# State-space levels of a hybrid trunk: eight places of a hand-written timetable, or four

## The chip, the cores and the metric

The kernel runs on one core of a Trainium2 chip. The metric is the device time of one execution in microseconds. It was run three times on the chip, and the median is compared; one more execution was recorded by the hardware profiler. Engines: TensorE (PE, with its weight loads shown apart as PEld), VectorE (DVE), ScalarE (ACT), GpSimd (POOL) and SyncE (SP), which here only issues DMAs.

## The reference, cut to what matters

One layer over 1024 frames of width 2048: RMSNorm, one input projection, three groups of heads (A: HGRN2, 6 heads; B: band attention, 5; C: retention, 5), each with a SiLU gate, one output projection, a residual and a last RMSNorm. The change touches group A only:

```
o_inter = einsum('bhtk,bhkv->bhtv', qn * exp(b), state)        # b = cumsum(log f)
diff    = b[:, :, :, None, :] - b[:, :, None, :, :]
decay   = exp(where(causal[:, :, None], diff, -inf))
scores  = einsum('bhtsk,bhsk->bhts', qn[:, :, :, None, :] * decay, kn)
o       = o_inter + einsum('bhts,bhsv->bhtv', scores, vn)
new_state = exp(b_last)[..., None] * state + einsum('bhsk,bhsv->bhkv', kn * exp(b_last - b), vn)
```

The decay between two frames differs per channel, so the scores aren't one matrix product. They are built by halving: for a block of 2n frames, the scores of the late half against the early half are a product of q * exp(b - b_mid) and k * exp(b_mid - b), with b_mid the last frame of the early half.

## The kernel before

The work is staged in three parts. First 30 of the 59 tiles of the input projection, with seven products in place of eight (Strassen's scheme, to about 598 us), then the other 29 tiles one by one, with the heads' own work laid between their matmuls (to about 1460 us), then the output projection, again with seven products. Everything is float32; a projection is three matmuls of split values (high x high, low x high, high x low), 512 columns each.

In the middle part `project(g, stages)` walks through a tile of weights in 16 rows; after every second row, which is 12 matmuls of 512 columns, it calls one entry of a list `stages`. Such a place is a *slot*; a tile has 8. `put(slot, *parts)` hangs parts into a slot, and they run on TensorE one after the other at the slot's end. This list is the timetable. TensorE issues in order, so a part whose semaphores are not there holds up the whole projection.

A head of group A begins at slot b = -4 + 20 u, u = 0 to 5, and has these parts on TensorE:

- `a_diag`: the diagonal blocks, 32 products of 32x32 outputs (64 instructions in the trace, each float32 product being two), into PSUM `mix[1]`.
- `a_level(u, n)`, n = 0 to 5, for halves of 64, 32, 16, 8, 4, 2 frames. Level 0 has 64-column tiles (16 instructions), level 1 has 32-column tiles (32), levels 2 to 5 have 32-column tiles (64). Even levels write `mix[0]`, odd ones `mix[1]`. The operands are in `LV[n % 2]`, two buffers in SBUF.
- `a_near`: neighbours one frame apart, two matmuls of 512 columns with a matrix of ones over a split vector (`part_sums`, L843 and L844), into `mix[0]`.
- `a_kdtr`, `a_state`, `a_out`, `a_ss`: transposes (L832), chunk states (L900), output (L911, L914), sums of squares.

The other engines work through an order of their own. For each level n VectorE does, in `a_unit`:

```python
                for n in range(NM):
                    if n + 2 < NM:
                        lv_diff_of(u, n + 2)
                    if n == 4:
                        near_diff_of(u)
                    lv_drain(u, n)
...
                    if n == 3:
                        dve.wait_ge(z1_in, 16 * (2 * u + 2))
                        silu_clamp(2 * u + 1)
                    if n + 2 < NM:
                        lv_mult(u, n + 2)
```

`lv_diff_of(u, n + 2)` (L1792, L1793) waits until TensorE has finished level n, whose operands it overwrites; ScalarE then takes the exponential (L1136), and `lv_mult` (L1800, L1802) forms the operands of level n + 2. `lv_drain` (L1846 for levels 0 and 1, L1853 for the others) copies a level's blocks out of PSUM. At n = 4 follow `near_diff_of` (L1809), `near_mult` (L1815, L1817), `silu_finish` (L1657) and `part_low` (L1822); the near stage waits for the last. The clamp (L1648) starts ScalarE's sigmoid of the gate: three passes, with near's exponential behind them. After level 5's drain come `near_drain` (L1832), the start of the next head and, once `a_state` is done, the states.

GpSimd meanwhile splits each arriving granule of projection weights into a high and a low part (L765, L767). A granule serves two slots; SyncE loads the next into its place when TensorE has done with it.

Of the kernel before, what the change touches and what calls it, by code (L numbers as in the profile page):

```python
# [134 lines left out]
def build(nc, xT, wi, w, wo, gain, lbl, hgain, relb, fgain, ident_d, level_d, start_d, rot_d, dec_d, outT):  # L135
# [4 lines left out]
    with ExitStack() as ctx:  # L140
# [69 lines left out]
        def blocks(n):  # L210
            return arena[:, n, :].rearrange("p (c t) -> p c t", c=BLK)
# [63 lines left out]
        def mixb(n):  # L275
            return mix[n][:, :].rearrange("p (c t) -> p c t", c=BLK)
# [502 lines left out]
        def _(pe):  # L779
# [42 lines left out]
            def fill(n, before):  # L822

                if not (isinstance(before, int) and before == 0):
                    pe.wait_ge(drained[n], before)
# [13 lines left out]
            def part_sums(out, use):  # L839


                pe.wait_ge(parts_split, use + 1)
                nc.tensor.matmul(out, ones[:], part_hi[:], start=True, stop=False)  # L843
                return nc.tensor.matmul(out, ones[:], part_lo[:], start=False, stop=True)  # L844

            def a_diag(u):
                def stage():
                    pe.wait_ge(rstd_ready, 3)
                    pe.wait_ge(k_ready, u + 1)
                    pe.wait_ge(silu_done, 2 * u + 1)  # L850
                    fill(1, A_M1 * u)
                    for c in range(BLK):
                        for at in range(0, P, ROWS):
                            last = nc.tensor.matmul(mixb(1)[at:at + ROWS, c, at:at + ROWS],
                                                    blocks(K)[:, c, at:at + ROWS], blocks(Q)[:, c, at:at + ROWS],
                                                    start=True, stop=True)
                    last.then_inc(filled[1], 1)
                return stage

            def a_near(u):  # L860
                def stage():
                    fill(0, A_M0 * u + 3)
                    part_sums(mix[0][:, 0:HALF], A_PARTS * u).then_inc(filled[0], 1)
                return stage

            def a_level(u, n):
                def stage():
                    m = n % 2
                    pe.wait_ge(lv_ready, 2 * (NM * u + n + 1))
                    fill(m, (A_M0 * u + n // 2) if m == 0 else (A_M1 * u + 1 + n // 2))  # L870
                    size = LEVELS[n]
                    for c in range(BLK):
                        if n < WIDE:
                            for early in range(0, P, 2 * size):
                                late = early + size
                                out_row = early + size * (c % 2)
                                last = nc.tensor.matmul(
                                    mixb(m)[out_row:out_row + size, c, late:late + size],
                                    blocks(LV[n % 2])[:, c, early:early + size],
                                    blocks(LV[n % 2])[:, c, late:late + size], start=True, stop=True)  # L880
                        else:
                            for at in range(0, P, ROWS):
                                part = blocks(LV[n % 2])[:, c, at:at + ROWS]
                                last = nc.tensor.matmul(mixb(m)[at:at + ROWS, c, at:at + ROWS], part, part,  # L884
                                                        start=True, stop=True)
                    last.then_inc(filled[m], 1)
                return stage

            def a_kdtr(u):
                def stage():  # L890
                    transposes(1, T3, kd_ready, u + 1, A_M1 * u + 4)
                    a_vtr(u)
                return stage

            def a_state(u):
                def stage():
                    pe.wait_ge(drained[1], A_M1 * u + 5)
                    pe.wait_ge(drained[0], A_M0 * u + 5)
                    for c in range(BLK - 1):
                        last = nc.tensor.matmul(mixb(1)[:, c, :], blocks(KDT)[:, c, :],  # L900
                                                blocks(V)[:, c, :], start=True, stop=True)
                    last.then_inc(filled[1], 1)
                return stage

            def a_out(u):
                def stage():
                    pe.wait_ge(drained[1], A_M1 * u + 6)
                    pe.wait_ge(qe_ready, u + 1)
                    fill(0, A_M0 * u + 5)
                    for c in range(BLK):  # L910
                        last = nc.tensor.matmul(mixb(0)[:, c, :], blocks(V)[:, c, :],  # L911
                                                blocks(SC)[:, c, :], start=True, stop=(c == 0))
                        if c > 0:
                            last = nc.tensor.matmul(mixb(0)[:, c, :], blocks(ST)[:, c, :],  # L914
                                                    blocks(QE)[:, c, :], start=False, stop=True)
                    last.then_inc(filled[0], 1)
                return stage
# [10 lines left out]
            def a_ss(u, half):  # L928
                return sum_squares(1, A_PARTS * u + 1, half, A_M1 * u + 6)
# [114 lines left out]
            def put(slot, *parts):  # L1044
                before = stages[slot]

                def stage():
                    before()
                    for part in parts:
                        part()  # L1050
                stages[slot] = stage

            for u in range(A_HEADS):
                b = A_FROM + A_EACH * u
                put(b + 7, a_diag(u))
                put(b + 8, a_level(u, 0))
                put(b + 9, a_level(u, 1))
                put(b + 11, a_level(u, 2))
                put(b + 12, a_level(u, 3))
                put(b + 13, a_level(u, 4))  # L1060
                put(b + 15, a_level(u, 5))
                put(b + 16, a_near(u))
                put(b + 17, a_kdtr(u))
                put(b + 18, a_state(u))
                put(b + 20, a_out(u))
                put(b + 22, a_ss(u, 0))
                put(b + 24 if u < A_HEADS - 1 else b + 23, a_ss(u, 1))
            for i in range(B_HEADS):
                b = B_FROM + B_EACH * i
# [3 lines left out]
            for i in range(C_HEADS - 1):  # L1073
                b = C_AT[i]
# [1265 lines left out]
```

## Time and profile before

| what | value |
| --- | --- |
| median of 3 runs | 1789.6 us (1788.89 to 1789.95) |
| profiled execution, its own time | 1790.76 us |
| its span, first to last instruction | 1789.0 us |
| mean granted TensorE clock | 0.993 of full speed |
| TensorE busy | 1745.5 us, 98% |
| VectorE busy | 1211.0 us, 68% |
| GpSimd busy | 766.8 us, 43% |
| ScalarE busy | 670.4 us, 37% |
| DMA, mean rate | 181 GB/s |

An engine that is busy for nearly all of the span sets the time; the others matter where that one waits for them. Matmuls overlap in the array, so the sum of their single durations is more than the busy time, and start-to-start distances are what prices a piece of work.

### The profile page before, as it was taken

What the parts mean: (1) busy time and instruction counts of PE and PEld (TensorE: products, weight loads), DVE (VectorE), ACT (ScalarE), POOL (GpSimd) and SP (SyncE); (2) the same over time, 40 slices, a digit from 0 to 9 for tenths busy, and PEclk for the clock granted to TensorE, in tenths of its full rate; (3) what the DMA queues carried; (4) which work ended last, traced back from release to release, by engine and by line L of the source; (5) the groups of instructions that cost most, each with busy time, mean ns of one, the idle gap of its engine ahead of it and who ended that gap; (6) DMA issues with size and microseconds to landing.
All of it is one profiled execution on the core that took longest, in us unless ns stands there. A gap on an engine that the chain in (4) does not pass through costs nothing.

```text
span 1789.0 us, 26920 instructions
## 1 busy us (share of the span) xinstructions
PE 1745.5 (98%) x10330; PEld 1443.2 (81%) x10330; DVE 1211.0 (68%) x1714; ACT 670.4 (37%) x972; POOL 766.8 (43%) x545
## 2 busy tenths in 40 slices
PE   7999999999999899999999999999999999999996
PEld 5888888888888788888887888888888877888884
DVE  6857565564678987787787356555655457778987
ACT  4423334332434253343443233332543223333442
POOL 4544444444455644444444333333333450354541
PEclk9999999999999999999999999999999999999997
DMA  7767777685987433224223332323433378778876
GB/s 247 228 229 252 242 239 255 218 269 184 301 270 247 153 99 109 89 84 123 85 84 124 108 108 84 106 84 106 145 109 110 97 247 307 234 241 261 287 241 223
DMA packets 160851, 323.29 MB, mean 181 GB/s; under 512 B 18378, under 2 KB 19151, under 8 KB 160724
## 3 DMA queue, kind: packets, MB, share of 16 engines
q1 hardware_dynamic: 146458, 276.52, 48.4%
q10 hardware_dynamic: 14266, 45.05, 7.3%
q8 instruction: 83, 1.36, 0.3%
q14 instruction: 44, 0.36, 0.1%
HBM read 275.35 MB, written 46.15 MB: 180 GB/s over the span
## 4 chain that ended last, share of the span: by engine, by line
PE 57%; DVE 5%; DMA 2%; issue 1%; ACT 1%; SPq 0%; POOL 0%; ACTq 0%; DVEq 0%
PE prj L813 33%; PE prj L1095 13%; PE mix L958 2%; PE mix L941 1%; DMA y_in<-y_scratch 1%; PE mix L832 1%; DVE arena L2276 1%; PE mix L951 1%; PE mix L884 1%; PE mix L911 1%; PE mix L914 1%; PE mix L900 1%; PE mix L989 0%; PE mix L1011 0%; DVE w_lo L2221 0%
## 5 line engine op out<-in xcount | busy, mean ns | idle before, releaser
L765 POOL TENSOR_SCALAR w_hi<-w_sum 128x512 fp32r<-128x512 f32 x124 | 198.9, 1604 | 514.2 <-DMA w_sum<-in_w 494.8
L792 PE MATMUL prj<-in_hi,w_hi 128*128 128x512 f32 x840 | 329.5, 392 | 10.7 <-DVE w_lo L1687 8.9
L792 PE MATMUL prj<-in_lo,w_hi 128*128 128x512 f32 x840 | 328.3, 391 | 0.0
L792 PE MATMUL prj<-in_hi,w_lo 128*128 128x512 f32 x840 | 328.2, 391 | 0.0
L813 PE MATMUL prj<-mv_hi,w_hi 128*128 128x512 f32 x928 | 300.6, 405 | 0.0
L752 POOL TENSOR_TENSOR w_sum<-in_raw,in_raw 128x512 f32<-128x512 f32 x150 | 200.0, 1334 | 214.4 <-PE prj L792 203.3
L813 PE MATMUL prj<-mv_lo,w_hi 128*128 128x512 f32 x928 | 288.4, 392 | 0.0
L813 PE MATMUL prj<-mv_hi,w_lo 128*128 128x512 f32 x928 | 286.4, 390 | 0.0
L813 PEld LDWEIGHTS prj<-mv_hi,w_lo 128*128 128x128 f32 x928 | 174.5, 188 | 38.8
L813 PEld LDWEIGHTS prj<-mv_lo,w_hi 128*128 128x128 f32 x928 | 174.5, 188 | 38.4
L792 PEld LDWEIGHTS prj<-in_hi,w_hi 128*128 128x128 f32 x840 | 158.5, 189 | 45.8 <-issue 9.4
L1687 DVE TENSOR_TENSOR w_lo<-w_sum,w_hi 128x512 fp32r<-128x512 f32 x150 | 119.0, 795 | 110.3 <-ACT w_hi L1198 108.4
L813 PEld LDWEIGHTS prj<-mv_hi,w_hi 128*128 128x128 f32 x928 | 163.9, 189 | 28.5 <-issue 0.9
L792 PEld LDWEIGHTS prj<-in_hi,w_lo 128*128 128x128 f32 x840 | 158.5, 189 | 33.3
L792 PEld LDWEIGHTS prj<-in_lo,w_hi 128*128 128x128 f32 x840 | 158.5, 189 | 33.1 <-issue 0.5
L774 POOL TENSOR_TENSOR raws<-raws 128x512 f32<-128x512 f32 x80 | 111.9, 1401 | 164.8 <-DMA raws<-in_wo 164.8
L1095 PE MATMUL prj<-mv_hi,w_hi 128*128 128x512 f32 x448 | 175.4, 391 | 6.4 <-POOL w_lo L767 4.1
L1136 ACT ACTIVATE arena<-arena 128x1024 f32<-128x1024 f32 (+1 forms) x121 | 123.6, 1034 | 151.2 <-DVE arena L1793 127.0
L767 POOL TENSOR_TENSOR w_lo<-w_sum,w_hi 128x512 fp32r<-128x512 f32 x124 | 173.8, 1402 | 10.3
L1095 PE MATMUL prj<-mv_lo,w_hi 128*128 128x512 f32 x448 | 174.4, 389 | 0.0
L1095 PE MATMUL prj<-mv_hi,w_lo 128*128 128x512 f32 x448 | 174.3, 389 | 0.0
L1198 ACT ACTIVATE w_hi<-w_sum 128x512 fp32r<-128x512 f32 x150 | 94.1, 628 | 178.2 <-POOL w_sum L752 178.0
(177 smaller groups left out, 2473.5 us busy)
## 6 DMA issues: line engine op xcount, KB each, us to landing
in_raw<-in_wi SPq DMA_DIRECT2D x360, 256.0 KB, 3.2
raws<-in_wo SPq DMA_DIRECT2D x184, 256.0 KB, 3.5
w_sum<-in_w SPq DMA_DIRECT2D x116, 256.0 KB, 2.9
arena<-z_scratch ACTq DMA_DIRECT2D x56, 512.0 KB, 4.0
y_in<-y_scratch SPq DMA_DIRECT2D x80, 256.0 KB, 4.5
z_scratch<-acc_in SPq DMA_DIRECT2D x60, 256.0 KB, 4.0
z_scratch<-stage SPq DMA_DIRECT2D x26, 512.0 KB, 4.2
x_even<-in_xT SPq DMA_DIRECT2D x44, 256.0 KB, 3.9
```

The lines of the kernel that those rows point to most:

```text
L752: nc.gpsimd.tensor_tensor(w_sum[wslot(n)][:], in_raw_buf(a), in_raw_buf(b), ALU.add if sign > 0 else ALU.subtract).then_inc(in_wsum, 1)
L765: nc.gpsimd.tensor_scalar(w_hi[q][:], w_sum[q][:], 1.0, None, ALU.mult).then_inc(w_hi_done, 1)
L767: nc.gpsimd.tensor_tensor(w_lo[q][:], w_sum[q][:], w_hi[q][:].bitcast(F32), ALU.subtract).then_inc(w_split, 1)
L774: nc.gpsimd.tensor_tensor(raw_buf(a), raw_buf(a), raw_buf(b), ALU.add if sign > 0 else ALU.subtract).then_inc(wsum_done, 1)
L792: last = nc.tensor.matmul(out, wt[wslot(n)][:, i % GRAN, :], mv[j % 2][:, i, :], start=(i == 0 and wt is w_hi and mv is in_hi), stop=(i == ...
L813: last = nc.tensor.matmul(prj[pair][:, half(side)], wt[wslot(q)][:, kk, :], mv[:, k, half(side)], start=(k == 0 and wt is w_hi and mv is m ...
L832: last = nc.tensor.transpose(mixb(n)[:, c, :], blocks(src)[:, c, :], ident[:])
L958: last = nc.tensor.matmul(mixb(1)[:, 5, :], blocks(V)[:, p + 1 - nk + j, :], blocks(BT[p % 2])[:, j, :], start=(j == 0), stop=(j == nk - 1))
L1095: last = nc.tensor.matmul(bank(s), wt[wslot(W0 + n)][:, i % GRAN, :], slot(mv, j, i), start=(i == 0 and wt is w_hi and mv is mv_hi), stop= ...
L1136: return nc.scalar.activation(out, src, ACT.Exp, **kw)
L1198: nc.scalar.activation(w_hi[wslot(n)][:], src, ACT.Copy).then_inc(in_w_hi, 1)
L1687: tt(w_lo[wslot(n)][:], src, w_hi[wslot(n)][:].bitcast(F32), ALU.subtract).then_inc(w_split, 1)
```

## The change

The eight parts of each head, from the diagonal to near, keep their order and their content. They are hung into fewer slots: the diagonal with level 0, level 1 with 2, level 3 with 4, level 5 with near, three slots apart. Nothing else of the kernel is edited.

```diff
             for u in range(A_HEADS):
                 b = A_FROM + A_EACH * u
-                put(b + 7, a_diag(u))
-                put(b + 8, a_level(u, 0))
-                put(b + 9, a_level(u, 1))
-                put(b + 11, a_level(u, 2))
-                put(b + 12, a_level(u, 3))
-                put(b + 13, a_level(u, 4))
-                put(b + 15, a_level(u, 5))
-                put(b + 16, a_near(u))
+                put(b + 7, a_diag(u), a_level(u, 0))
+                put(b + 10, a_level(u, 1), a_level(u, 2))
+                put(b + 13, a_level(u, 3), a_level(u, 4))
+                put(b + 16, a_level(u, 5), a_near(u))
                 put(b + 17, a_kdtr(u))
                 put(b + 18, a_state(u))
                 put(b + 20, a_out(u))
```

## Rows read from the trace of the kernel before

**Rows 1.** The page: busy us, share of the span and instructions of an engine.
```profile
PE 1745.5 (98%) x10330; PEld 1443.2 (81%) x10330; DVE 1211.0 (68%) x1714; ACT 670.4 (37%) x972; POOL 766.8 (43%) x545
```

**Rows 2.** TensorE's waits: for whom, us in total, times, longest.
```profile
PE mix L884 <- DVE arena L1802: 4.6, 2, 3.0
```

**Rows 3.** Windows: length, busy of PE, PEld, DVE, ACT, POOL; clock, DMA share, GB/s.
```profile
618.00:621.00 3.00, 0.02 (x1) 0.00 (x0) 3.00 (x4) 0.00 (x0) 2.92 (x3) 0.96 0.00 0
621.00:623.00 2.00, 1.97 (x66) 1.78 (x67) 2.00 (x2) 0.00 (x0) 1.63 (x2) 0.50 0.00 0
728.00:797.00 69.00, 69.00 (x677) 56.67 (x676) 53.35 (x72) 27.73 (x31) 30.38 (x20) 1.00 0.30 93
```

**Rows 4.** The chain of work that ended last: start, us, three slots of projection.
```profile
803.57 8.16 PE prj L813 x36
```

**Rows 5.** Timeline of weight loads, head 3, then level 3 of head 4: start, duration.
```profile
811.65 0.65 PEld L854 LDWEIGHTS mix<-arena 128*32 128x32 f32 x64 [0.35 <-issue]
815.31 0.55 PEld L877 LDWEIGHTS mix<-arena 128*64 128x64 f32 x16 [0.35 <-issue]
818.87 0.35 PEld L877 LDWEIGHTS mix<-arena 128*32 128x32 f32 x32 [0.35 <-issue]
824.93 0.65 PEld L884 LDWEIGHTS mix<-arena 128*32 128x32 f32 x64 [0.35 <-DVE arena L1802]
828.59 0.65 PEld L884 LDWEIGHTS mix<-arena 128*32 128x32 f32 x64 [0.35 <-issue]
832.25 0.65 PEld L884 LDWEIGHTS mix<-arena 128*32 128x32 f32 x64 [0.35 <-issue]
838.63 0.65 PEld L884 LDWEIGHTS mix<-arena 128*32 128x32 f32 x64 [0.35 <-issue]
841.97 0.19 PEld L843 LDWEIGHTS mix<-part_hi,ones 128*128 128x128 f32 x1
...
897.28 0.65 PEld L884 LDWEIGHTS mix<-arena 128*32 128x32 f32 x64 [0.35 <-issue]
```

**Rows 6.** Timeline of VectorE, head 3, from level 3's end to near.
```profile
829.48 1.10 DVE L1792 TENSOR_TENSOR arena<-arena 128x512 f32<-128x512 f32 x1
...
832.35 0.67 DVE L1648 TENSOR_SCALAR arena<-arena 128x1024 f32<-128x1024 f32 x1
...
836.86 0.69 DVE L1815 TENSOR_TENSOR arena<-arena 128x512 f32<-128x512 f32 x1 [0.77 <-ACT arena L1136]
837.58 1.66 DVE L1817 TENSOR_TENSOR arena<-arena 128x512 f32<-128x512 f32 x1
...
840.30 0.68 DVE L1822 TENSOR_TENSOR part_lo<-arena,part_hi 128x512 fp32r<-128x512 f32 x1
```

**Rows 7.** Timeline of VectorE, head 1, the same stretch, first and last.
```profile
692.52 0.68 DVE L1792 TENSOR_TENSOR arena<-arena 128x512 f32<-128x512 f32 x1
...
703.59 0.68 DVE L1822 TENSOR_TENSOR part_lo<-arena,part_hi 128x512 fp32r<-128x512 f32 x1
```

**Rows 8.** Timeline of VectorE, head 0, the same stretch, first and last.
```profile
625.70 0.69 DVE L1792 TENSOR_TENSOR arena<-arena 128x512 f32<-128x512 f32 x1
...
635.17 0.68 DVE L1822 TENSOR_TENSOR part_lo<-arena,part_hi 128x512 fp32r<-128x512 f32 x1
```

**Rows 9.** Timeline of weight loads, head 0: levels 2, 3, 4 and near.
```profile
614.30 0.65 PEld L884 LDWEIGHTS mix<-arena 128*32 128x32 f32 x64 [2.04 <-DVE arena L1802]
621.03 0.95 PEld L884 LDWEIGHTS mix<-arena 128*32 128x32 f32 x64 [3.44 <-DVE arena L1802]
625.95 0.65 PEld L884 LDWEIGHTS mix<-arena 128*32 128x32 f32 x64 [0.35 <-DVE arena L1802]
...
635.97 0.19 PEld L843 LDWEIGHTS mix<-part_hi,ones 128*128 128x128 f32 x1 [0.33 <-issue]
```

**Rows 10.** Timeline of GpSimd, head 3: one half of each of two weight splits.
```profile
829.02 1.89 POOL L765 TENSOR_SCALAR w_hi<-w_sum 128x512 fp32r<-128x512 f32 x1 [3.19 <-DMA w_sum<-in_w]
...
837.17 1.52 POOL L767 TENSOR_TENSOR w_lo<-w_sum,w_hi 128x512 fp32r<-128x512 f32 x1
```

## The prediction

> **What bounds the kernel now.** I read the page's busy table first. TensorE is busy for 98% of the span [rows 1], so the time is TensorE's queue plus its waits. The view of the waits, for TensorE alone, then says how much of them belongs to the six A heads: only 4.6 us in two waits, both ahead of a level (L884) and both for VectorE's multiply L1802 [rows 2]. The windows show one whole head, 728 to 797 us: TensorE has work for 69.00 of 69.00 us at full clock, VectorE for 53.35 [rows 3]. So in heads 1 to 5 each microsecond in which TensorE issues or waits more is a microsecond of the total; in head 0 it is VectorE that leads.
>
> The timeline of weight loads prices a stage. A slot of projection is 8.16 / 3 = 2.72 us [rows 4]. From the diagonal blocks to level 0 is 3.66 us, from level 3 to level 4 is 3.66, from level 4 over two slots to level 5 is 6.38 [rows 5]: a stage of 64 small matmuls adds 0.94. Level 1 has 32 and adds 824.93 - 818.87 - 5.44 = 0.62. So a small matmul costs 0.01 us and the stage, as a stage, 0.30. Each of them starts with an idle 0.35 on the loader, for 128x32 tiles and for 128x64 ones alike; the near stage, on the whole array, starts with none [rows 5].
>
> **The change, part by part.** No instruction, transfer or buffer is added or removed. What is issued where changes on TensorE only; the orders on VectorE, ScalarE, GpSimd and SyncE's queue stay. Against the head's start b: level 0 moves from b+8 to b+7, level 1 from b+9 to b+10 (later), level 2 from b+11 to b+10 (earlier), level 3 from b+12 to b+13 (later), level 4 stays, level 5 moves from b+15 to b+16 (later), near stays.
>
> *Gain.* Levels 1 and 2 follow each other with the same tile shape, as do 3 and 4: each seam saves the 0.30 of a stage. Level 5 and near save nothing, since near never paid. The diagonal and level 0 differ in shape (128x32, then 128x64), and no row has such a pair: nothing saved is one bound, 0.30 the other. The idle 0.35 appears whenever the array goes from whole to narrow tiles and must come from the shape, since the near stage waits on semaphores too and has none; I take 0.10, near the lower bound, because the tile shape changes here as well. (The Trainium skill, "TensorEngine Tiling (Array Packing)", Key Properties, says that changing the tiling mode drains TensorE. By that rule the seam saves nothing and the sum ends 0.5 us higher; with the row's price counted as fully saved it would be 1.0 us lower. The idle 0.35 ahead of narrow stages agrees with the rule.)
>
> *What the later levels cost.* VectorE's queue is in order. Behind its wait for level 3 stand: the differences for level 5 (L1792, L1793), level 3's drain, the clamp L1648, the products for level 5, near's difference L1809, level 4's drain, near's products L1815 and L1817, the gate L1657 and the split L1822. TensorE's near stage waits for the last of these. I call the stretch from L1792 to the end of L1822 the chain. It took 840.98 - 829.48 = 11.50 us in head 3 [rows 6], 704.27 - 692.52 = 11.75 in head 1 [rows 7] and 635.85 - 625.70 = 10.15 in head 0 [rows 8]. Between the start of level 3 and near TensorE had 13.38 us before [rows 5]: the chain starts 0.89 after level 3, ends 12.39 after it in head 3, and fits.
>
> Now near comes after level 3 by: 0.64 (level 3's matmuls) + 0.94 (level 4 as a stage) + 8.16 (three slots) + 0.62 (level 5; 841.97 - 838.63 - 2.72) = 10.36 us. The chain needs 0.89 + 10.15 + 0.12 = 11.16 at its shortest (0.12: from the chain's end to near's start in head 0 [rows 8, 9]). So near waits in every head: at least 0.8 us.
>
> How long is the chain? Of the 4.51 us from the clamp to L1815 [rows 6], all is ScalarE's (three passes for the sigmoid, one for near); the VectorE work under it has 3.7 us and so 0.8 us of slack. The rest, 5.6 us, is plain VectorE work that GpSimd's splits of the projection weights stretch: L1792 took 1.10 instead of 0.69 beside L765 [rows 6, 10], L1817 took 1.66 instead of 0.69 beside L767, and began anew only when L767 was through at 838.69. GpSimd's pair starts some 3.4 us after an odd slot frees its weights. Level 3 will stand right behind an odd slot, so a pair falls 3 to 6 us into the stage, mostly under ScalarE's part: it costs what exceeds the slack, I take 0.4. The next falls 10 us in, on the gate or the split: 0.3. Chain: 10.15 + 0.7 = 10.85. Bounds: 10.15 (no collision) and 11.75 (as head 1).
>
> *Sum for a head.* From near to the next head's level 3 it was 897.28 - 841.97 = 55.31 [rows 5]; it becomes 55.31 + 2.72 - 0.30 - 0.10 = 57.63. From there to near 0.89 + 10.85 + 0.12 = 11.86, a wait of 1.5. The period is 69.49 instead of 68.69 (897.28 - 828.59): +0.80. The seam between levels 3 and 4 is inside the wait and is worth nothing.
>
> *Head 0.* VectorE is busy for 3.00 of 3.00 us while level 3 waits [rows 3, 9], and it has level 1 and level 2 as early as it needs them in either order. Level 2 will wait some 5 us in one piece at 609 to 614 us instead of 1.7 and 3.1 in two, and level 4 will start when the products for it are done, 625.9 as now [rows 9]. Its near at 635.97 was already set by the chain. So head 0 keeps its time: 0 (from -1.1, if a weight split misses VectorE, to +0.4).
>
> Five periods from near to near: 5 x 0.80 = +4.0 us. After head 5's near every stage stands at its old slot, and near's drain and level 5's end ahead of the transposes a slot later, so the shift is passed on whole. The profiled execution took 1790.8 us (span 1789.0), 1.2 over the median of the runs: 1789.6 + 4.0 = 1793.6.
>
> Other waits checked: level 4 needs the products for it, 7.96 us after level 1 starts (VectorE: 0.55, then three steps of each of two levels at 1.2 to 1.35), and comes after 10.0; a collision or two fit. If not, level 4 is later and near's wait shorter by as much. Level 2 needs its own 5.5 us after the diagonal and comes after 9.9.
>
> **The rivals.**
> 1. *The chain meets no weight split.* 10.15 us, +0.10 a head, +0.5 in all: 1790.1. For it: head 0 ran so. Against it: all of heads 1 to 5 were longer, and a pair of splits comes with every second slot.
> 2. *The chain is as long as before.* 11.75: +1.70 a head, 1798.1. For it: five heads had 11.5 to 11.8. Against: level 3 now stands elsewhere against the splits.
> 3. *The wait pulls the clock down.* In head 0 a wait of 3.1 us was followed by a granted clock of 0.50 for 621 to 623 us [rows 3, 9], and the slot behind it took 4.92 instead of 3.66: 1.26 lost. The wait of 1.7 us at 614.30 cost no clock. Near's wait would be 1.5, but idle 0.3 and a stage of small matmuls stand right ahead of it. If it counts, 5 x 1.26 more: 1799.9.
> 4. *Faster: near doesn't wait.* If what near needs were ready within 10.36 us of level 3, the three seams would be pure gain: 5 x 0.9 = 4.5, 1785.1. It decides at a chain of 9.35 us, 0.8 below the shortest one seen.
> 5. *Nothing changes*, because a stage's 0.30 isn't lost at its boundaries but in its matmuls: then the period is 0.4 longer than in the forecast, 1795.6.
>
> **How the numbers follow.** About 0.2% (3.6 us) is what a measurement of this kernel can tell from no change. Forecast, a chain of 10.5 to 11.3: 0.60, with a range of its own of 1791.8 to 1796; rival 1: 0.15; rival 2: 0.08; rival 3: 0.07; rival 4: 0.05; rival 5: 0.05. 1793.6 lies just beyond 0.2% (1793.2), so of the forecast 0.34 is slower and 0.26 the same. Slower: 0.34 + 0.08 + 0.07 + 0.05 = 0.54. Same: 0.26 + 0.15 = 0.41. Faster: 0.05. The range from 1789.8 to 1798.5 leaves out rivals 3 and 4 and the better end of rival 1.
>
> **What would show it.** In the profile after, for heads 1 to 5: a start-to-start of 0.3 us from level 1 to level 2 and 0.6 from 3 to 4, with no idle between; some 0.5 to 0.8 from the diagonal to level 0; TensorE waiting at near's first matmul (L843) for L1822, five times 0.8 to 2.4 us; a period of 69.5; level 2 of head 0 waiting 5 us. Wrong it would be if the chain were under 10.2, if the waits stood at level 4 instead, or if the granted clock left 1.00 in the heads.

## The result, and the profile after

The changed kernel takes 1798.07 us (median of 5 runs, 1796.48 to 1800.84), the kernel before 1789.95 (5 runs, 1788.89 to 1793.3). The ratio is 1.0046, with a 95% interval from 1.0035 to 1.0057: 8.1 us slower, where the forecast was 4.0 us slower. The profiled execution took 1797.53 us, its span is 1795.7.

The waits of TensorE alone, in the kernel after (line, for whom, us in total, times, longest). Lines of the file behind the timetable stand four earlier than before: L1818 is L1822 of before, L1798 is L1802.

```profile
PE mix L843 <- DVE part_lo L1818: 9.5, 6, 3.0
PE prj L792 <- DVE w_lo L1683: 8.2, 1, 8.2
PE mix L884 <- DVE arena L1798: 5.9, 1, 5.9
```

The first row did not exist before: near now waits in each of the six heads. The second belongs to the start of the kernel and was 8.9 us before. The third is head 0; the 4.6 us in two waits of [rows 2] have become 5.9 in one.

The timeline of weight loads in head 4, to be held against [rows 5]:

```profile
884.74 0.65 PEld L854 LDWEIGHTS mix<-arena 128*32 128x32 f32 x64 [0.35 <-issue]
885.43 0.55 PEld L877 LDWEIGHTS mix<-arena 128*64 128x64 f32 x16
894.43 0.35 PEld L877 LDWEIGHTS mix<-arena 128*32 128x32 f32 x32 [0.35 <-issue]
894.67 0.70 PEld L884 LDWEIGHTS mix<-arena 128*32 128x32 f32 x64
903.82 1.25 PEld L884 LDWEIGHTS mix<-arena 128*32 128x32 f32 x128 [0.35 <-issue]
913.50 0.65 PEld L884 LDWEIGHTS mix<-arena 128*32 128x32 f32 x64 [0.35 <-issue]
915.89 0.19 PEld L843 LDWEIGHTS mix<-part_hi,ones 128*128 128x128 f32 x1 [1.75 <-issue]
```

All three seams are free of the idle 0.35. Near starts 2.39 us after level 5, where 0.64 would do: 1.75 us of waiting, though the row calls it "issue" and only the view of the waits names L1818. (Single waits at near are given below as this idle time of the loader; the view of the waits has them 0.1 us shorter.) From level 3 to near it is 12.07 us.

What near waits for, on VectorE in the same head, to be held against [rows 6]:

```profile
904.62 0.69 DVE L1788 TENSOR_TENSOR arena<-arena 128x512 f32<-128x512 f32 x1 [1.59 <-PE mix L884]
...
907.05 1.12 DVE L1644 TENSOR_SCALAR arena<-arena 128x1024 f32<-128x1024 f32 x1
...
909.30 1.78 DVE L1805 TENSOR_TENSOR arena<-arena 128x512 f32<-128x512 f32 x1
...
912.23 0.67 DVE L1811 TENSOR_TENSOR arena<-arena 128x512 f32<-128x512 f32 x1
...
914.68 1.10 DVE L1818 TENSOR_TENSOR part_lo<-arena,part_hi 128x512 fp32r<-128x512 f32 x1
```

And GpSimd beside it, to be held against [rows 10]:

```profile
907.02 1.62 POOL L765 TENSOR_SCALAR w_hi<-w_sum 128x512 fp32r<-128x512 f32 x1 [2.85 <-DMA w_sum<-in_w]
908.73 1.81 POOL L767 TENSOR_TENSOR w_lo<-w_sum,w_hi 128x512 fp32r<-128x512 f32 x1
914.03 2.08 POOL L765 TENSOR_SCALAR w_hi<-w_sum 128x512 fp32r<-128x512 f32 x1 [3.49 <-DMA w_sum<-in_w]
```

Ahead of the chain VectorE now stands idle for 1.59 us until level 3 is through; then it has 915.78 - 904.62 = 11.16 us of work in one piece, in which three operations are stretched: the clamp (1.12 instead of 0.67) by L765, near's difference (1.78 instead of 0.67) by L767, the split (1.10 instead of 0.68) by the next L765.

The granted clock fell in two waits of TensorE and stayed at 0.50 behind them, at near of head 1, which starts at 707.18, and at level 2 of head 0, at 613.11 (columns as in [rows 3]):

```profile
707.00:709.00 2.00, 1.79 (x4) 1.49 (x5) 1.84 (x5) 0.00 (x0) 0.00 (x0) 0.50 0.69 244
709.00:711.00 2.00, 2.00 (x7) 1.55 (x6) 1.97 (x5) 0.00 (x0) 0.00 (x0) 0.67 0.02 6
...
612.00:615.00 3.00, 1.89 (x66) 1.74 (x67) 2.94 (x7) 0.71 (x1) 3.00 (x1) 0.50 0.02 5
615.00:617.00 2.00, 2.00 (x6) 1.52 (x6) 1.96 (x4) 0.35 (x1) 1.92 (x3) 0.50 0.00 0
```

Where the 6.7 us between the two spans lie, by four starts on TensorE, each read from the timeline of weight loads:

| stretch | before | after | difference |
| --- | --- | --- | --- |
| start to the diagonal of head 0 | 599.34 | 597.03 | -2.3 |
| from there to near of head 0 | 36.63 | 39.36 | +2.7 |
| near of head 0 to near of head 5 | 343.39 | 348.40 | +5.0 |
| from there to the end | 809.6 | 810.9 | +1.3 |

The change touches nothing in the first stretch. Over the profiled executions of all the kernels below it ran from 596.7 to 599.4, and the last one from 806.8 to 813.8: both vary by more than what they show here. So the two middle rows, 7.7 us, are what the change did in this trace, and the 8.1 us of the medians agree.

### The profile page after: what moved, and what is told of

Read it like the earlier page. It is cut to its first block, busy times and chain, and to the rows that moved or that the text cites. A ratio compares the mean times of both kernels' runs of the same rounds, so it can differ in the third digit from the quotient of the medians.

```text
span 1795.7 us, 26920 instructions
## 1 busy us (share of the span) xinstructions
PE 1741.8 (97%) x10330; PEld 1446.3 (81%) x10330; DVE 1203.7 (67%) x1714; ACT 669.2 (37%) x972; POOL 778.1 (43%) x545
## 4 chain that ended last, share of the span: by engine, by line
PE 54%; DVE 7%; issue 2%; DMA 2%; ACT 1%; SPq 0%; POOL 0%; ACTq 0%; DVEq 0%
PE prj L813 30%; PE prj L1091 13%; PE mix L958 2%; PE mix L941 1%; PE mix L832 1%; DVE arena L2272 1%; PE mix L951 1%; DMA y_in<-y_scratch 1%; ACT arena L1132 1%; PE mix L911 1%; PE mix L914 1%; PE mix L900 1%; PE mix L1011 0%; PE mix L989 0%; PE mix L884 0%
## 5 line engine op out<-in xcount | busy, mean ns | idle before, releaser
L765 POOL TENSOR_SCALAR w_hi<-w_sum 128x512 fp32r<-128x512 f32 x124 | 202.5, 1633 | 516.5 <-DMA w_sum<-in_w 497.1
L752 POOL TENSOR_TENSOR w_sum<-in_raw,in_raw 128x512 f32<-128x512 f32 x150 | 203.8, 1359 | 208.3 <-PE prj L792 197.9
L1683 DVE TENSOR_TENSOR w_lo<-w_sum,w_hi 128x512 fp32r<-128x512 f32 x150 | 114.9, 771 | 110.1 <-ACT w_hi L1194 107.4
L767 POOL TENSOR_TENSOR w_lo<-w_sum,w_hi 128x512 fp32r<-128x512 f32 x124 | 175.2, 1413 | 10.3
```

The lines of the kernel that those rows point to most:

```text
L752: nc.gpsimd.tensor_tensor(w_sum[wslot(n)][:], in_raw_buf(a), in_raw_buf(b), ALU.add if sign > 0 else ALU.subtract).then_inc(in_wsum, 1)
L765: nc.gpsimd.tensor_scalar(w_hi[q][:], w_sum[q][:], 1.0, None, ALU.mult).then_inc(w_hi_done, 1)
L767: nc.gpsimd.tensor_tensor(w_lo[q][:], w_sum[q][:], w_hi[q][:].bitcast(F32), ALU.subtract).then_inc(w_split, 1)
L1683: tt(w_lo[wslot(n)][:], src, w_hi[wslot(n)][:].bitcast(F32), ALU.subtract).then_inc(w_split, 1)
```

## The experiments

Each was timed beside the kernel before on the same chip. The lines of the timetable are those of the changed kernel if nothing else is said. For each the table gives what the traces show; a stage of 64 small matmuls added 0.90 us in these executions instead of 0.94, so the 343.39 of before answers to about 342.5 here, as the two controls have it. The new timetable shows no such difference: from near to the next head's level 3 it is 57.4 us in the changed kernel's own trace and in head0_old.

| kernel | diagonal to near, head 0 | near of head 0 to near of head 5 | near's waits, heads 1 to 5 | chain, mean of heads 1 to 5 | ratio to before (95%) |
| --- | --- | --- | --- | --- | --- |
| before | 36.63 | 343.39 | 0 | 11.69 | 1 |
| changed | 39.36 | 348.40 | 5 | 11.09 | 1.0046 (1.0035 to 1.0057) |
| level3_back | 37.57 | 340.38 | 0 | 11.21 | 0.9990 (0.9978 to 1.0002) |
| level3_only | 38.02 | 348.33 | 5 | 10.87 | 1.0049 (1.0032 to 1.0066) |
| gate_early | 38.34 | 339.89 | 1 | 9.36 | 0.9989 (0.9978 to 1.0001) |
| gate_early_before | 38.24 | 342.47 | 0 | 10.72 | 0.9997 (0.9985 to 1.0008) |
| head0_old | 36.62 | 347.17 | 5 | 11.11 | 1.0026 (1.0016 to 1.0037) |
| small_splits | 37.16 | 342.22 | 5 | 10.13 | 0.9978 (0.9968 to 0.9988) |
| small_splits_before | 32.46 | 342.46 | 0 | 10.16 | 0.9947 (0.9934 to 0.9960) |
| head0_level2 | 39.00 | 347.53 | 5 | 11.20 | 1.0049 (1.0033 to 1.0066) |
| best | 36.81 | 339.88 | 1 | 9.42 | 0.9981 (0.9972 to 0.9990) |

**Level 3 back by one slot.**

```diff
-                put(b + 13, a_level(u, 3), a_level(u, 4))
+                put(b + 12, a_level(u, 3))
+                put(b + 13, a_level(u, 4))
```

> The changed kernel with level 3 of each head put back one slot (b+12), level 4 alone at b+13. Theory (the VectorE chain from level 3's end to near's split sets near, and moving level 3 one slot later is what made near wait): near's waits in heads 1 to 5 go away, the seams diagonal/level 0 and level 1/level 2 stay, a period from near to near of 68.69 - 0.25 - 0.36 = 68.1 us instead of the 69.7 mean after, head 0 still loses about 2 us. Total about 1789 to 1792, some 6 to 9 us below the changed kernel. Rival (two levels back to back on TensorE cost by themselves, wherever they stand): only the seam between levels 3 and 4 is gone, about 1795 or more.

1790.11 us (12 runs). The waits at near are gone from the view of the waits, and the period is 68.02 to 68.11 us in all five heads, as expected. Head 0 loses 0.9 us, where about 2 were expected. In head 1:

```profile
690.93 0.65 PEld L884 LDWEIGHTS mix<-arena 128*32 128x32 f32 x64 [0.35 <-issue]
694.55 0.65 PEld L884 LDWEIGHTS mix<-arena 128*32 128x32 f32 x64 [0.35 <-issue]
703.61 0.65 PEld L884 LDWEIGHTS mix<-arena 128*32 128x32 f32 x64 [0.35 <-issue]
704.38 0.19 PEld L843 LDWEIGHTS mix<-part_hi,ones 128*128 128x128 f32 x1
```

13.45 us from level 3 to near, over a chain that is as long as in the changed kernel (a mean of 11.21 beside 11.09). The rival, that two levels in a slot cost by themselves, is refuted: two of the seams are still there and are a gain of 2 us over the control's 342.5. (The pair of levels 3 and 4 stands again in gate_early below, and costs nothing there.) In the total this gain can't be told from none, with head 0's loss beside it.

**Only level 3 moved**, in the kernel before:

```diff
-                put(b + 12, a_level(u, 3))
-                put(b + 13, a_level(u, 4))
+                put(b + 13, a_level(u, 3), a_level(u, 4))
```

> The kernel before with one edit alone: level 3 of each head one slot later, at b+13 with level 4. Theory: this alone brings near's waits. From near to the next level 3 58.0 us, from there to near about 12.0, a period of 70.0 instead of 68.7, 5 x 1.3 = 6.5 us slower than before, about 1796; head 0 keeps its two smaller waits at levels 2 and 3 and loses little. Rival (the loss comes from levels 1 and 2 in one slot): no wait at near, within 1 us of before.

1799.56 us (6 runs). One part moved by one slot gives as large a loss as the whole change. TensorE waits at near in heads 1 to 5, 5.7 us by the view of the waits, and the periods are 68.95 to 70.18. The size was missed: about 6.5 us were expected, and the ratio is worth 8.8. In the trace the five periods have 348.3 - 342.5 = 5.8 of it and head 0 1.4, where TensorE waits 4.0 us at level 4 and the granted clock is 0.50 behind that wait.

```profile
694.55 1.25 PEld L884 LDWEIGHTS mix<-arena 128*32 128x32 f32 x128 [0.35 <-issue]
701.55 0.65 PEld L884 LDWEIGHTS mix<-arena 128*32 128x32 f32 x64 [0.35 <-issue]
706.79 0.19 PEld L843 LDWEIGHTS mix<-part_hi,ones 128*128 128x128 f32 x1 [1.97 <-issue]
```

**The gate's clamp and sigmoid earlier.** On VectorE the clamp moves from level 3's step to level 1's, on ScalarE the sigmoid from behind level 5's exponential to ahead of it:

```diff
-                    if n == 3:
+                    if n == 1:
                         dve.wait_ge(z1_in, 16 * (2 * u + 2))
                         silu_clamp(2 * u + 1)
...
-                sigmoid(2 * u + 1)
+                    if n == 4:
+                        sigmoid(2 * u + 1)
```

> The changed kernel, with the gate's clamp on VectorE moved from level 3's step to level 1's, and the gate's sigmoid on ScalarE moved ahead of level 5's exponential. The same work, but 4.5 us of ScalarE's are no longer between the clamp and near's products. Theory: the chain from level 3's end to near's split falls to about 8.7 to 9.5 us, near no longer waits (it has 9.4), and the seams become pure gain, 0.95 a head: period 67.7, 5 us faster than before; head 0 gets back some 1 to 2 us. Total 1784 to 1788. Rival (near waits because VectorE is short of time, not for the path through ScalarE): the chain stays near 11 us and the total near 1798.

1788.39 us (11 runs). The chain is 9.1 us in four heads and 10.40 in head 3, the only one of the five in which near waits (0.98 us). VectorE in head 1, the whole chain:

```profile
694.52 0.70 DVE L1789 TENSOR_TENSOR arena<-arena 128x512 f32<-128x512 f32 x1 [1.01 <-PE mix L884]
695.15 0.67 DVE L1790 TENSOR_TENSOR arena<-arena 128x512 f32<-128x512 f32 x1
695.76 1.32 DVE L1850 COPY_PREDICATED arena<-level,mix 128x1024 f32<-128x1024 int8 x1
...
697.02 0.69 DVE L1797 TENSOR_TENSOR arena<-arena 128x512 f32<-128x512 f32 x1
697.63 1.10 DVE L1799 TENSOR_TENSOR arena<-arena 128x512 f32<-128x512 f32 x1
698.65 0.68 DVE L1806 TENSOR_TENSOR arena<-arena 128x512 f32<-128x512 f32 x1
699.26 1.34 DVE L1850 COPY_PREDICATED arena<-level,mix 128x1024 f32<-128x1024 int8 x1
...
700.49 0.67 DVE L1812 TENSOR_TENSOR arena<-arena 128x512 f32<-128x512 f32 x1
701.20 0.69 DVE L1814 TENSOR_TENSOR arena<-arena 128x512 f32<-128x512 f32 x1
701.81 1.22 DVE L1654 SCALAR_TENSOR_TENSOR arena<-arena 128x1024 f32<-128x1024 f32 x1
702.94 0.69 DVE L1819 TENSOR_TENSOR part_lo<-arena,part_hi 128x512 fp32r<-128x512 f32 x1
```

Near starts at 704.13 right behind level 5, half a microsecond after the split is there. With the gate taken out of the chain, it fits under three slots: from head 0's near to head 5's it is 8.5 us shorter than in the changed kernel (7.3 shorter than in head0_old, where the clock does not fall), and the seams are now a gain. What left the chain is not only the path through ScalarE. In heads 1, 3 and 4 of the changed kernel VectorE has no wait for ScalarE at near's products (L1811); there the clamp itself is gone, 1.0 to 1.1 us, and the splits meet near's difference in head 3 alone (1.78; 0.68 above). In heads 2 and 5 a wait of 0.38 and 0.34 is gone as well. The edit moves both halves of the gate, so these runs don't price them singly. The part of the expectation on head 0 was nearly right: 38.34 after 39.36, 1.0 us back where 1 to 2 were expected. The sum was not reached: the total was to be 5 us faster than before and at most 1788.0 us, and by its interval the median can't be told from the kernel before.

The same edit in the kernel before, as the control:

> The kernel before with the same move of the gate's clamp and sigmoid, the timetable untouched. Theory: near does not wait in the kernel before, so a shorter chain is worth nothing: the period stays 68.7, within 1 us of before. Rival (the gate's place costs something of its own): it moves by more than 2 us, and then the run of the changed kernel with this edit can't be read as the timetable's gain.

1790.87 us (12 runs), no difference from before: the periods are 68.49 to 68.50 and near has no wait to lose. In head 0, where VectorE leads, the earlier clamp stands ahead of level 3's products: level 3 comes 0.7 us later, the clock stays low for longer behind its wait, and the head takes 1.6 us more (38.24). So what gate_early gains over this control, 2.6 us of 342.5 in the heads, is the timetable's.

**Head 0 alone on the old timetable** (eight `put` lines of before for u = 0, the four of after for the others).

> The changed kernel, but head 0 alone keeps the eight places of before. Theory (head 0 loses because its one wait of 5.5 us at level 2 is followed by a low clock that makes level 3 late for VectorE): from the diagonal to near 36.6 us in head 0 instead of 39.35, the other heads as in the changed kernel, total 2 to 3 us below it, about 1795 to 1797. Rival (head 0's difference is only its weight splits falling elsewhere): it stays at 38 or more.

1795.84 us (12 runs): head 0 takes 36.62 us, exactly as before, and the total is 0.20% of the kernel's time nearer to before (ratios 1.0026 and 1.0046), as expected. So the change costs head 0 2.7 us in the trace, and heads 1 to 5 the rest. All five wait at near, 1.18 to 1.88 us, and in none of them the granted clock leaves 1.00: the sum is 347.2 - 342.5 = 4.7 us.

**GpSimd's operations cut to a sixteenth.** This kernel and its control leave out work: of each granule of the middle part GpSimd treats 8 of 128 columns of each row, and the third product of the projection reads the high part of the weights, so the 29 tiles are computed with wrong weights.

```diff
-                nc.gpsimd.tensor_scalar(w_hi[q][:], w_sum[q][:], 1.0, None, ALU.mult).then_inc(w_hi_done, 1)
+                few = slice(0, P) if n < IN_GRANULES + NG or n >= W0 else slice(0, 8)
+                nc.gpsimd.tensor_scalar(w_hi[q][:, :, few], w_sum[q][:, :, few], 1.0, None, ALU.mult).then_inc(w_hi_done, 1)
...
-                    for wt, mv in ((w_hi, mv_hi), (w_hi, mv_lo), (w_lo, mv_hi)):
+                    for third, wt, mv in ((0, w_hi, mv_hi), (0, w_hi, mv_lo), (1, w_hi, mv_hi)):
```

> The changed kernel with GpSimd's two operations on the weights of the middle part cut to 8 of 128 columns a row; the third product of the projection reads the high part instead of the low one, so all 29 tiles of the middle part are computed with wrong weights, with the same matmuls. Theory (weight splits stretch the chain from 10.15 to 11.07 on average): all five chains 10.0 to 10.3 us, near's wait 0.7 to 0.9 each, near to near about 68.5 to 68.7 a head and no low clock, 5 us less than the changed kernel from head 0's near to head 5's. Rival (collisions aren't what differs between the chains): they still spread from 10.1 to 12.4.

1787.45 us (12 runs). The six chains are 10.12 to 10.15 us long, as head 0's of [rows 8]; near waits 0.67 to 0.71 in each head, the periods are 68.42 to 68.47, both at or just under the low end of what was expected. The five periods are 6.2 us shorter than in the changed kernel, where 5 were expected, and 5.0 shorter than in head0_old. In head 1, the chain's ends:

```profile
692.96 0.69 DVE L1789 TENSOR_TENSOR arena<-arena 128x512 f32<-128x512 f32 x1 [2.00 <-PE mix L885]
...
699.92 0.69 DVE L1812 TENSOR_TENSOR arena<-arena 128x512 f32<-128x512 f32 x1 [0.71 <-ACT arena L1133]
...
702.39 0.69 DVE L1819 TENSOR_TENSOR part_lo<-arena,part_hi 128x512 fp32r<-128x512 f32 x1
```

ScalarE ends later than VectorE here (0.71 us of waiting at near's products): without collisions the path through the sigmoid sets this part of the chain. In the changed kernel it does so in heads 2 and 5 only, and in heads 1, 3 and 4 VectorE's own stretched work does. All that the six chains differ by is GpSimd's work beside them.

> The same cut of GpSimd's operations in the kernel before, as a control. Theory: near has room there, so the period stays 68.5 to 68.7 in heads 1 to 5; head 0, which VectorE leads, shortens by 2 to 4 us from diagonal to near. Rival: heads 1 to 5 shorten as well, and then the splits cost TensorE something else.

1782.51 us (6 runs). Heads 1 to 5 keep 342.46, so the splits cost TensorE nothing where the chain has room. Head 0 falls from 36.63 to 32.46. Against this control the change costs heads 1 to 5 nothing (342.22) and head 0 4.7 us, and the two medians differ by 4.9.

The pair says something of head 0 too. Its chain is as short in both, 10.15 and 10.14 us, and still the change costs it 4.7 us. TensorE and VectorE at its level 3, in small_splits:

```profile
612.00 0.95 PEld L885 LDWEIGHTS mix<-arena 128*32 128x32 f32 x64 [4.30 <-DVE arena L1799]
623.71 1.25 PEld L885 LDWEIGHTS mix<-arena 128*32 128x32 f32 x128 [0.35 <-issue]
...
624.52 0.69 DVE L1789 TENSOR_TENSOR arena<-arena 128x512 f32<-128x512 f32 x1 [3.95 <-PE mix L885]
```

Behind a wait of 4.2 us the clock stands at 0.50 for 612 to 617 us, level 3 follows level 2 after 11.71 us instead of the 9.13 of the other heads, and VectorE stands idle for 3.95. So no collision is needed for head 0 to lose: a late level 3 is enough.

**Level 2 of head 0 one slot later.**

```diff
-                put(b + 10, a_level(u, 1), a_level(u, 2))
+                put(b + 10, a_level(u, 1))
+                put(b + 11 if u == 0 else b + 10, a_level(u, 2))
```

> The changed kernel with level 2 of head 0 alone put one slot later (b+11), so that TensorE has 2.7 us of projection to do before it waits for it. Theory (in head 0 the long wait at level 2 lowers the clock, level 3 comes 2.2 us late and VectorE, ready 1.7 us earlier, waits for it): the wait falls from 5.7 to about 3 us, at most 1.3 us are lost to the clock, level 3 is there before VectorE is, the VectorE wait of 1.7 us for it is gone and the diagonal-to-near time of head 0 falls from 39.35 to about 37.7 us, up to 1 us either way by where weight splits fall. Rival (only the weight splits differ): it stays above 39.

1798.48 us (4 runs), and 39.00 us from diagonal to near: the expected 37.7 was missed. VectorE's wait for level 3 is gone, as the theory has it, but what was to follow did not:

```profile
615.58 0.76 PE L884 MATMUL mix<-arena 128*32 128x32 f32 x64 [2.81 <-DVE arena L1799]
616.27 1.12 PE L813 MATMUL prj<-mv_hi,w_hi 128*128 128x512 f32 x2
617.18 1.05 PE L813 MATMUL prj<-mv_lo,w_hi 128*128 128x512 f32 x2
```

The wait of 2.8 us lowered the clock like the one of 5.9 (0.50 for 617 to 619 us); VectorE was through with the products for level 4 1.5 us later than in the changed kernel, counted from the diagonal, of which about 1.1 are operations that weight splits stretched; and TensorE waited another 2.8 us at level 4 and lost clock again behind it. That the old timetable cures head 0 is shown, and by small_splits that it loses without collisions too; how the 2.7 us of the changed kernel divide between a late level 3 and the splits is not.

**The version that these runs point to**: the four places and the early gate for heads 1 to 5, head 0 as in the kernel before.

```diff
-                    if n == 3:
+                    if n == (1 if u > 0 else 3):
```

and the same condition at the sigmoid (4 or 5).

> Heads 1 to 5 with the four places and the gate's clamp and sigmoid early, head 0 with everything as before. Theory: head 0 36.6 us from diagonal to near, a period of 67.8 in the others, near waiting at most once; 0.9 x 5 = 4.5 us faster than before, about 1785 to 1787. Rival (what is gained in the heads is given back behind them): below 1 us faster.

1787.88 us (12 runs) beside 1791.75 for the kernel before: 0.19% faster, the interval from 0.10 to 0.28%. The periods are 67.8, 68.7 in head 3. Expected were 4.5 us; in the heads the trace has 342.5 - 339.9 = 2.6, by the controls, and the medians differ by 3.9. The miss is in the price of the seams: with no wait a period is 67.79 instead of 68.49, so the new places are worth 0.7 a head and not 0.9, and head 3 loses more than that in a wait of 1.0.

## Why the prediction was right, point by point

The direction, the place and the cause of the loss were right. The size was not: 8.1 us instead of 4.0. The range held by 0.4 us (1798.07, its end is 1798.5), and that is partly luck: the end was set for a longer chain (rival 2), and what filled the difference are two terms that the sum had at nothing, head 0 (2.7 us) and one fall of the clock (1.4).

- *Near waits for VectorE's chain in every head, since level 3 comes one slot later.* Right, and shown from both sides: level3_back takes the waits away, level3_only brings them by itself, and a chain of 9.1 us (gate_early) makes them vanish, where the prediction had put the turning point at 9.35; the one head with a longer chain there (10.40) waits.
- *The chain, 10.85 us between 10.15 and 11.75.* Measured 12.48, 10.14, 11.05, 11.16 and 10.60, mean 11.1. The shortest agrees with the lower bound; head 1 went over the upper one, because five of its operations were stretched. The collisions were the unknown, taken as 0.7, and are 0.9. The forecast had the clamp free of them; it was stretched by up to 0.45 in three heads, ahead of ScalarE's part, where nothing hides it.
- *The seams, 0.30 + 0.10 outside the wait.* Level 2 now starts 0.25 us after level 1, where level 1 had been priced at 0.62: 0.36 saved, of which level 2 gives 0.04 back. The diagonal and level 0 follow at 0.69 us without the idle 0.35, and that saves 0.25. (The Trainium skill, "TensorEngine Tiling (Array Packing)", Key Properties, has any change of the tiling mode drain TensorE. This trace shows no such cost for 128x32 to 128x64: the idle 0.35 came only from the whole array to narrow tiles.) With 0.07 for level 5 and near, which the forecast had at nothing, it was 57.4 us from near to the next level 3, not 57.63.
- *The clock.* The forecast left it out of near's waits and gave it a rival of its own, with 0.07. It came once of five: in head 1, behind a wait of 3.0 us, near to the transposes took 4.54 instead of 3.1. The waits of 0.7 to 1.75 us in the others, and of up to 1.9 in head0_old, cost none.
- *Heads 1 to 5: 4.0 us.* Measured 5.0: 1.4 of it the clock, the rest 3.6, so that without the clock the sum was close. head0_old, without that fall, has 4.7; the 1.1 between the two is nearly all in what they are held against (343.4 and 342.5), since 348.4 - 1.4 and 347.2 are alike.
- *Head 0: no change.* This is the step that failed. It costs 2.7 us. The one long wait at level 2 was foreseen, with its place and length (5 us; the view of the waits has 5.9). But the prediction took VectorE as the one that leads head 0 throughout, and put nothing for when TensorE would reach level 3; the low clock it weighed at near alone. That clock made level 3 come 11.27 us after level 2 instead of the 9.1 of the other heads, and VectorE, ready earlier, waited 1.66 us for it; the chain behind was 11.10 instead of 10.15. 1.7 + 0.95 is about the 2.7 by this reading of the trace. small_splits shows the first half without the second, but the one run meant to separate the two here did not.
- *The signs of being wrong.* Two of the prediction's own came up, in one head each: the chain of head 2 was under 10.2 (10.14, with a wait of 0.7 behind it), and the clock left 1.00 in head 1. Neither changes the cause, but head 1's wait of 3.1 us and head 2's of 0.7 lie outside the 0.8 to 2.4 that were named.
- *The other waits* (level 4, level 2 of heads 1 to 5) did not arise, and what stands behind near kept its place.

## What to carry to other kernels

When a part is moved in a timetable, look not at the part but at the first thing that is queued behind it on another engine and has a deadline of its own: here level 3 had slack, its end opened a chain of 11 us, and near had 0.2 to 0.9 us left. A seam saved is worth 0.2 to 0.3 us, a slot lost to a chain 2.7; take from the chain first (here the gate's clamp on VectorE and ScalarE's three passes, which nobody needed there), then tighten the timetable. And a stretch that another engine leads is not free ground: in head 0 two waits of 1.6 and 3.0 us had cost 1.3 us of clock ahead of level 4, for which VectorE was only just ready; the one of 5.9 cost 2.1 ahead of level 3, for which VectorE then waited.

## What was unexpected of the hardware

- A switch from 128x32 to 128x64 tiles shows no idle time (0.69 us from the first of 64 matmuls to the next shape), from the whole array to either 0.35.
- Where it falls whole on a VectorE operation, a weight split stretches it by one of two amounts: an operation of two SBUF inputs by 0.4 beside the tensor-scalar (1.10 for 0.68), by 1.1 beside the tensor-tensor (1.78), and the clamp, a tensor-scalar of one input, from 0.67 to 1.12 beside the first and to 1.77 beside the second (head 0 of gate_early_before). (The Trainium skill, "SBUF — State Buffer", Who interferes with whom, says that such operations take turns at a shared port and that the later one waits for the whole of the earlier one. The 1.78 agrees: the operation ends 0.54 us after L767. The 1.10 doesn't: in head 4 it was over at 915.78, while the L765 ahead of it ran to 916.11.)
- Of the waits of TensorE in the heads, those up to 1.8 us (by the view of the waits) left the start-to-start distances behind them as they were; those of 2.8 us and more were followed by lengthened ones and by a granted clock of 0.50. None lay between.
